# Expert weights on two DMA queues, a slot table made on chip, and empty slots left out of the row transfers

## The reference, cut to what matters

```
x  = x + mixed @ w_out
h2 = rmsnorm(x)
group  = argmax over 8 of (h2 @ w_rg + b_rg)             # top-1 group
2 experts of the group's 8 by (h2 @ w_re + b_re)         # top-2
wts = softmax over the two, times the group's probability
y  = sum over the 2 of wts * ((silu(h2 @ w_gate[e]) * (h2 @ w_up[e])) @ w_down[e])
out = rmsnorm(x + y)
```

## Time and profile before

| | us |
|---|---|
| median of 3 runs | 1718.99 (1711.0 to 1719.74) |
| the profiled execution's own time | 1719.11 |
| its span | 1717.2 |
| mixer, to the last transposes of mixed | 977 |
| w_out, routing, to the first turn_x | 977 to 1128 |
| expert loop | 1128 to 1681 |
| tail | 1681 to 1717.2 |
| mean granted TensorE clock | 0.901 of full |

### The profile page before, as it was taken

The page is one execution under the profiler, slowest core; times in us unless marked ns, Lnnn a source line. Parts: engine busy times, 40 slices in busy tenths (PEclk is TensorE's granted clock), DMA queues, the critical chain, the costliest instruction groups (busy, mean ns, idle before and its releaser), DMA issues.

```text
span 1717.2 us, 20700 instructions
## 1 busy us (share of the span) xinstructions
PE 1419.1 (83%) x6772; PEld 809.0 (47%) x6772; DVE 822.1 (48%) x1718; ACT 334.2 (19%) x901; POOL 205.3 (12%) x301
## 2 busy tenths in 40 slices
PE   5799999999999999999999698267786878778780
PEld 4458567475574755757557543222222222222220
DVE  2286575866857657577476323512222122212224
ACT  3122122232231312313123201001111111101112
POOL 2210121101211111101111000210000000000002
PEclk9899899999989989999899699579988898989895
DMA  8931030210302103021012320359999999999985
GB/s 187 193 100 38 26 87 15 61 38 26 87 14 62 38 26 86 3 74 38 26 25 110 122 87 25 150 210 421 421 423 421 423 422 423 421 423 422 422 366 181
DMA packets 127246, 306.61 MB, mean 179 GB/s; under 512 B 15564, under 2 KB 89254, under 8 KB 102246
## 3 DMA queue, kind: packets, MB, share of 16 engines
q1 hardware_dynamic: 111750, 258.87, 40.1%
q0 software_dynamic: 8800, 27.52, 4.5%
q10 hardware_dynamic: 6672, 19.93, 4.1%
HBM read 272.45 MB, written 34.83 MB: 179 GB/s over the span
## 4 chain that ended last, share of the span: by engine, by line
PE 61%; DMA 23%; DVE 7%; issue 3%; ACT 3%; SPq 1%; POOL 0%; POOLq 0%; ACTq 0%; DVEq 0%
DMA arena<-in_w_up 22%; PE PB L1081 13%; PE PB L1099 10%; PE PB L1415 8%; PE PB L1105 7%; PE PB L1359 4%; PE PB L1183 2%; PE PB L1211 2%; PE PB L1076 2%; DVE arena L1561 1%; PE PB L1074 1%; PE PB L1299 1%; PE PB L1290 1%; PE PB L1125 1%; PE PB L1038 1%
## 5 line engine op out<-in xcount | busy, mean ns | idle before, releaser
L1415 PE MATMUL PB<-arena 128*64 128x512 f32 x1024 | 269.3, 675 | 115.7 <-DMA arena<-in_w_up 111.8
L1081 PE MATMUL PB<-arena 128*128 128x512 f32 x512 | 224.0, 595 | 0.0
L1415 PEld LDWEIGHTS PB<-arena 128*64 128x64 f32 x1024 | 76.7, 154 | 282.6 <-issue 143.3
L1914 DVE TENSOR_SCALAR arena<-arena 128x256 f32<-128x256 f32 x32 | 9.4, 295 | 383.5 <-ACT arena L953 383.5
L1105 PE MATMUL PB<-arena 128*128 128x128 f32 x1280 | 169.4, 288 | 6.2 <-ACT arena L841 5.5
L1099 PE MATMUL PB<-arena 128*128 128x384 f32 x512 | 170.8, 487 | 0.0
L1105 PEld LDWEIGHTS PB<-arena 128*128 128x128 f32 x1280 | 158.4, 201 | 14.7 <-ACT arena L841 7.4
L902 ACT ACTIVATE arena<-PB 128x512 f32<-128x512 f32 (+3 forms) x116 | 60.0, 521 | 483.8 <-PE PB L1423 256.1
L1081 PEld LDWEIGHTS PB<-arena 128*128 128x128 f32 x512 | 96.0, 190 | 118.6 <-issue 118.1
L1099 PEld LDWEIGHTS PB<-arena 128*128 128x128 f32 x512 | 95.4, 190 | 63.2 <-issue 3.8
L1435 PE MATMUL PB<-arena 128*64 128x512 f32 x512 | 116.9, 598 | 1.1 <-ACT arena L902 1.1
(11 more groups left out here) (412 smaller groups left out, 1994.7 us busy)
## 6 DMA issues: line engine op xcount, KB each, us to landing
arena<-in_w_gate SPq DMA_DIRECT2D x64, 1024.0 KB, 19.4
arena<-in_w_up SPq DMA_DIRECT2D x64, 1024.0 KB, 21.5
arena<-in_w_down SPq DMA_DIRECT2D x64, 1024.0 KB, 25.2
arena<-in_w_in SPq DMA_DIRECT2D x58, 512.0 KB, 6.3
ye_d<-arena ACTq DMA_DIRECT2D x32, 512.0 KB, 8.1
Sb<-in_state_dn SPq DMA_DIRECT2D x8, 512.0 KB, 4.1
ye_d<-arena SPq DMA_DIRECT2D x2, 2048.0 KB, 8.9
out<-Sb POOLq DMA_DIRECT2D x8, 512.0 KB, 3.9
```

The lines of the kernel that those rows point to most:

```text
L1081: last = mm(PB[g][:, :], wch[:, c, g, :], hT[:, c, 0:TP], start=c == 0, stop=c == KC - 1)
L1415: last = mm(gu_bank[a][half[k], :], xT[:, a, c, half[k]], wgu[a][:, k, :, c, :], start=c == 0, stop=c == KC - 1)
```

## The change

There are six edits.

1. The expert loop's up loads move from SP to ACT. ACT issues the two of pair j+3 inside follow(j), after the exponential of pair j+1 and before it copies the transposed rows of pair j+2. SP keeps gate and down, and waits once for `s_ov_done` ahead of its second group of loads.
2. The slot table is made on chip. One-hot masks of the rank (`oh`) times one-hot masks of the expert scaled by (token number + 1) give, by small matmuls into PB[2], the number of the token in each slot and 0 in an empty one. `row_numbers` turns that into two index lists: `gidx` for the gather and `yidx` for the store. An empty slot has the index 4095 and is out of bounds in both.
3. Gathers get `bounds_check=T - 1, oob_is_err=False`. The store of the results is now an indirect scatter by POOL, out of bounds for empty slots, into `y2_d`, where row t (first choice) or 1024 + t (second) belongs to a token. The junk fill of `ye_d` is gone.
4. The overflow blocks still use a table in HBM; its arithmetic (`overflow_slots`) and the pair weights (`pair_weights`) move on DVE behind turned(0, 1), inside the start of the expert loop, and POOL's 10 small scatters go behind its first four gathers.
5. In the routing stage `ranks(n)` and `slot_table(n)` are done tile by tile, ACT's `stats(n)` goes ahead of its copy for tile n-1, DVE's resid(n) and h2_rows(n) go ahead of logits(n-1) and choose(n-1), and out_rows(4) is cut in four groups of 256 columns whose 32 output rows lie in four partition groups of one bank.
6. In the tail SP loads both rows of each token with one direct DMA per tile into five buffers, and no store waits for the one before.

```
+            def up_weights(it, a):
+                j = it * 2 + a
+                act.wait_ge(s_gu_ps, 1 + j)
+                for k in range(2):
+                    act.dma_start(wgu[a][:, k, 1, :, :], w_up[ds(it * 4 + (2 * a + k)), :, :]...).then_inc(gu_in[a], 16)
-            def follow(it, a, nxt=True, turn=True):
+            def follow(it, a, nxt=True, turn=True, up=True):
                 hid_turned(it, a)
                 if nxt:
                     exp_gate(*later(it, a, 1))
+                if up:
+                    up_weights(*later(it, a, 3))
                 if turn:
                     turned(*later(it, a, 2))
                 rows_out(it, a)
...
+            def gather(it, a):
+                j = it * 2 + a
+                pool.wait_ge(s_xt_ps, 1 + j * 2)
+                pool.tensor_copy(gidx2[:, a:a + 1], gidx[:, ds(j)]).then_inc(s_idx_ready, 1)
...
+                pool.indirect_dma_start(X[:, a, :], None, h2_d[:, :], bass.IndirectOffsetOnAxis(ap=gidx2[:, a:a + 1], axis=0),
+                                        bounds_check=T - 1, oob_is_err=False).then_inc(X_in[a], 16)
+            def scatter(it, a):
...
+                pool.indirect_dma_start(y2_d[:, :], bass.IndirectOffsetOnAxis(ap=yidx2[:, a:a + 1], axis=0), ys[:, a, :], None,
+                                        bounds_check=2 * CODE - 1, oob_is_err=False).then_inc(ye_out[a], 16)
+            for j in range(4):
+                gather(j // 2, j % 2)
+            pool.wait_ge(s_ov_done, 1)
+            (10 indirect DMAs into slot_d)
+            with pool.Fori(0, NPAIR // 2 - 2) as it:
+                for a in range(2):
+                    gather(it + 2, a)
+                    scatter(it, a)
...
+            def slot_table(n):
+                pe.wait_ge(s_oh_done, n + 1)
+                for k in range(2):
+                    for a in range(2):
+                        last = mm(PB[2][CAP * a:CAP * a + CAP, 0:NPAIR], oh[:, n, k, :], M[:, n, 3 + k, a:NE:2], ...)
...
             for n in range(NT):                       # PE
                 out_rows(n)
+                if n >= 2:
+                    ranks(n - 2)
                 if n:
                     route_rows(n - 1)
+            for n in range(NT - 2):
+                slot_table(n)
             route_rows(NT - 1)
+            ranks(3), ranks(4), slot_table(3), slot_table(4)
...
+                    for q in range(4):                # out_rows(4)
+                        last = mm(PB[0][32 * q:32 * q + 32, 0:256], hT[:, c, TP:T], wo[:, c, q * 256:(q + 1) * 256], ...)
...
+            for n in range(NT):                       # ACT
+                stats(n)
+                if n:
+                    h2_turned(n - 1)
...
             turned(0, 1)                              # DVE
+            pair_weights()
+            overflow_slots()
...
+            for n in range(NT):                       # SP, tail
+                sp.dma_start(yg[0:R, n, :, :], y2_rows[n * P:n * P + R, :, :]).then_inc(yg_in[min(n, 2)], 16)
```

More of the change, by code:

```diff
@@ L562, in _ @@
                 load_down(0, k, k)
-            sp.wait_ge(s_route_done, 1)
             def gate_up_weights(it, a):
@@ L577, in _ @@
                 gate_up_weights(it, 0)
+                sp.wait_ge(s_ov_done, 1)
                 down_weights(it - 1, 1)
@@ L925, in _, with stats @@
                 cpa(hT[:, 0:4, n * P:n * P + R], PB[2 * (n % 2)][:, :].rearrange("p (c k) -> p c k", c=4)[:, :, 0:R]).then_inc(s_mT_act, 1)
-            for n in range(NT):
+            def stats(n):
                 R = rows_of[n]
@@ L991, in further @@
                 rows_out(it, a)
[L993 to L997, removed]
+            further_blocks(act, further)
             for n in range(NT):
@@ new lines, in _, with row_numbers @@
+            resid(0)
+            h2_rows(0)
+            for n in range(1, NT):
+                resid(n)
+                if n >= 2:
+                    one_hot_ranks(n - 2)
+                h2_turned(n - 1)
+                h2_rows(n)
+                logits(n - 1)
+                if n == NT - 1:
+                    h2_turned(n)
+                choose(n - 1)
+            logits(NT - 1)
+            choose(NT - 1)
+            one_hot_ranks(NT - 2)
+            one_hot_ranks(NT - 1)
+            def row_numbers(v, em, sf, th, o):
+                step(ts(em, v, 0.0, 4.0 * CODE, ALU.is_equal, ALU.mult))
+                ch.inc(stt(sf, v, -1.0, em, ALU.add, ALU.add))
+                step(ts(th, v, CODE + 1.0, -1.0 * CODE, ALU.is_ge, ALU.mult))
+                ch.inc(cp(yidx[:, o], sf))
+                step(tt(gidx[:, o], sf, th, ALU.add))
+                dve.sem_inc(s_route_done, 1)
@@ L1837, in _ @@
+            cnt, ova, ovb, ov, adj, eb, ec = (e64[:, k, :] for k in range(1, 8))
+            dve.wait_ge(s_rk_ps, NT + 1)
+            row_numbers(PB[2][:, 0:NPAIR], adj[:, 0:NPAIR], adj[:, NPAIR:], eb[:, 0:NPAIR], slice(0, NPAIR))
+            ch.inc(cp(rkS[:, 0:NP, :].rearrange("p n e -> p (n e)"), PB[4][:, 0:NP * 64]))
+            step(cp(rkS[:, NP:, :].rearrange("p n e -> p (n e)"), PB[3][:, 0:128]))
+            cnt = rkS[:, NT, :]
             step(ts(ov, cnt, float(CAP), None, ALU.is_gt))
@@ L1937, in _ @@
             turned(0, 1)
-            with dve.Fori(0, NPAIR // 2 - 1) as it:
+            pair_weights()
+            overflow_slots()
+            for a in range(2):
+                follow(0, a)
+            with dve.Fori(1, NPAIR // 2 - 1) as it:
                 for a in range(2):
@@ L1947, in further @@
                 rows_out(it, a)
+            dve.wait_ge(s_slots_moved, 32)
+            step(cp(ovf[:, 0, :], ovraw[:, :]))
+            row_numbers(*(ovf[:, k, :] for k in range(4)), slice(NPAIR, NBLK // 2))
             further_blocks(dve, further)
```

324 lines of the change are left out of this document (170 added, 154 removed).

## The result

The kernel after takes 1662.05 us in the median (1659.5 to 1663.34), the kernel before 1719.37 beside it: ratio 0.9672, 95% interval 0.9636 to 0.9708. The forecast was 1630 with a range of 1604 to 1660. The direction was right, the size too large: 57 us are gained where 89 were forecast, and the time lies 2 us past the range. The profiled execution has a span of 1661.6 us.

A forecast was written before the change was run, and what follows sets the result against it. The prediction took DMA to bound the expert loop at about 422 GB/s. Its terms, -55.6 - 30.7 + 3.5 + 1 - 7.4 = -89.2, took 1719.1 to 1630 us, with a range of 1604 to 1660.

The forecast's parts named there:

- What bounds the loop: Expert loop: DMA bounds it at about 422 GB/s, 34.8 us a turn, and keeps the bound after the change.
- at 422 GB/s 55.6 us: Expert loop: skipping empty slots saves 23.5 MB of gathers and stores, 55.6 us; bounds 0 and 55.6.
- POOL's 10 scatters (12.7 us) are hidden: Start of the expert loop: the small scatters cost nothing, since gather(4) is wanted 20 us later.
- the hole of DMA: Start of the expert loop: DMA idle from about 21.5 to 25 us after turn_x(0), +3.5 us, bounds 0 and 8.
- Edit 6, the tail, -7.4: Tail after the loop: shortened from 33.1 to 25.7 us, so -7.4, bounds -10 and -4.
- DVE without a break: Tail: after issue and first tile, VectorE runs its steps without stopping, 20.3 us.
- The routing stage, -30.7: Routing ahead of the loop: -32.5 - 5.4 + 7.2 = -30.7 us, bounds -46 and -21; turn_x(0) at 1097.
- Edit 1, 0: Expert loop: issuing up loads from ACT gains 0, as the DMA engines are never out of work.
- the store from POOL, +1: Result stores issued by POOL: 0 in the loop, about +1 us once at the last pair.
- A: Rival for gathers and stores: out-of-bounds rows are moved or replaced all the same; 1686 us, chance 0.10.
- C: Rival in the loop: ACT is held inside its own DMA issues, slower than before; 1772 us, chance 0.04.
- B: Rival in the loop: three queues with work at once slow the engines to 400 GB/s; 1656 us, chance 0.07.

The follow-up runs named there:

- e7: Kernel after, with a bound on the ten small scatters so nearly all their 4-byte writes are left out: 1646.95 us, ratio 0.9583.
- e1: Kernel after without POOL's ten small scatters of the overflow table and their wait: 1644.96 us, ratio 0.9575.
- e8: Kernel after with ranks spread over the slots, the small scatters' writes bounded and a semaphore for every tile of the tail: 1632.83 us, ratio 0.9494.
- e4: Kernel before with only the up loads moved to ACT: 1716.17 us, ratio 0.9994.
- e2: Kernel after with the up loads back on SyncE, behind the gate loads: 1667.55 us, ratio 0.9689.
- e3: Kernel after without the ten small scatters, up loads back on SyncE, and the final norm's weight loaded ahead of the tail's tiles: 1654.71 us, ratio 0.961.
- e9: Kernel after with spread ranks, bounded scatters, a semaphore per tail tile, and up loads back on SyncE: 1636.91 us, ratio 0.9525.
- e5: Kernel after with an expert's ranks spread over its 64 slots by a table in place of the iota: 1649.69 us, ratio 0.9583.
- e6: Kernel after with ranks packed, eight in a row on the eight partitions of one engine: 1693.5 us, ratio 0.9833.

## Why the prediction was too low

1. **What bounds the loop.** Right, with a gap: DMA bounds it before and after. The text measured DMA as one resource of 422 GB/s. It behaves as sixteen of 26.4, and the turn ends with the busiest.
2. **Edit 3, "at 422 GB/s 55.6 us".** This is the step that failed. The bytes were right (27% of each transfer moves), the size was not: the sentence "The rate must not fall with the mix" rested on weights alone, which load all engines alike. In the kernel after the filled rows sit on some eight to ten engines. A turn took 32.5 us and not 31.05. Spreading the same rows took 12.5 us off the loop (15 to 20 by the expectation), packing them added 29.1 (33 by the expectation). The text gave this term the bounds 0 and 55.6, but its range took it at 55.6 throughout; with any smaller part of it the range would have had to reach further up.
3. **Edit 4, "POOL's 10 scatters (12.7 us) are hidden".** The second failed step. GpSimd's time is hidden, as the text says, and the hole of DMA that it forecast at +3.5 is there (326 and 289 GB/s from 1107 to 1127 us make 20 - (13 x 326 + 7 x 289) / 422 = 5.2 us). But the writes were costed by their bytes, at nothing, and slowed everything beside them: 9.7 us (e7) to 12.4 (e1). The wait for `s_ov_done` came as forecast: SyncE's down loads went out 29.5 us after turn_x(0), 29 by the text.
4. **Edit 6, the tail, -7.4.** It gave 33.1 - 29.2 = 3.9. "DVE without a break" was wrong: the third tile waited 2.82 us, since three tiles share one semaphore, and the first step came 7 us after the first issue and not 5.4. With one semaphore per tile the end comes 2.8 us sooner (e8).
5. **The routing stage, -30.7.** turn_x(0) came within 2 us (1095.12 against 1097), in part by luck: the stage began 2.0 us later than in the kernel before. From out_rows(0) on it took 108.5 us and not 143.4, so -34.9. The stalls behind stats are 2.35 to 2.78 us, as costed at 2.4. The clock behind them was not costed: out_rows(2) and (3) take 15.64 and 15.29 us for 13.95, at a granted clock of 0.89 and 0.91, 3.0 us more. out_rows(4) took 5.97 us and not 8.5, and most of that at the lower clock; by the estimate of 3.6 us at the full clock four groups do run abreast, which the text priced at 3.5 and did not take. The Trainium skill's "TensorE: Matmul & The Clock Gate", section "Part 3: Packing small matmuls", from which the text estimated 4.4 us, is nearer to that than the value taken. The stretch behind choose(4) gave 2.6 us more than forecast (1085.79 to 1095.12, 9.3 us and not 11.9).
6. **Edit 1, 0.** Right in the kernel before (e4, 0.9994). In the kernel after, two queues fill a hole at the loop's start worth 2.5 to 6 us of the loop (e2, e3, e9), which the text did not see: with one queue the up loads stand behind the wait for `s_ov_done` that edit 4 brought.
7. **Edit 3, the store from POOL, +1.** Nothing in the loop waits for it in any trace. Right in kind.
8. **The rivals.** A is out: q0 moved 5.74 MB in 20 pairs. C is out: ScalarE's issues took 348 ns. B has the right time, 1656 against 1662, by a wrong mechanism. Its rate of 400 GB/s is what the steady part shows, but not for the number of queues: one queue gives 409 (e2), and two queues with spread rows give 418 (e5).
9. **The sums.** Two do not come out quite. The stated bounds of the terms add up to 1608 to 1648 and not 1604 to 1650, and the steps of the tail to 20.2 and not 20.3. Neither changes the account.

The loop's 32.8 us over the forecast are then: imbalance and scatters together 534.8 - 511.6 = 23.2 (e8, with both gone), and 9.6 that remain in e8. Of these, 418 against 422 GB/s over some 470 us make 4.5, and the hole of 1107 to 1127, 4.5 us in e8 by the same working as in point 3, makes 1. Whether the 418 come from the engines that still have 3 rows where others have 2 or from the packets of skipped rows, no run here separates. The packet records give the second a size: in e8 some 3800 skipped rows of 9 ns are 35 of 5232 engine-us, 0.7%, where 418 lacks 1% of 422 (an estimate). The last 4 us are open.

## What to carry to other kernels

When an indirect transfer leaves rows out, ask where the remaining rows lie. The turns here went by the busiest of sixteen engines, so spread valid rows over all partition groups; one table of ranks did it, for 12 us. Some thousand 4-byte writes to HBM cost 10 to 12 us beside a stream of weights, though their issue was hidden: bound them, as e7 does, or try them in a quiet stage or on chip. A wait added to a queue holds up everything behind it, not only the load that needs it. Where a new order makes TensorE wait, look at its granted clock behind the wait too. And a sum of bytes over a mean rate should be checked once per engine before it is trusted.

## What the runs showed of the hardware

- A skipped (out-of-bounds) row of an indirect DMA moves no bytes but keeps its packet: 145 packets a transfer with 34 of 128 rows filled. q0's packets of 40 transfers took 5.1% of 5232 us, with the moved rows.
- Which partitions are filled is worth 44 us between e5 and e6, at equal instructions and bytes. The packed order was laid out by the assignment that e6's expectation names, and gave the time of eight rows on the busiest engine, as that assignment asks.
- 1088 writes of 4 bytes, in ten scatters, doubled the mean time of the weights' packets beside them (0.28 to 0.59 us), over some 20 us, and landed after 12.0 us. The median 8 KB packet stayed at 0.31 us, and 98 of 715 took 1 to 4.46 us.
- Four groups of 32-row matmuls, 64 records of 256 columns, took 5.97 us at a granted clock of 0.60, some 3.6 at the full clock, where the same columns in 32 records of 512, one after the other, took 13.85 at 1.00: 3.8 times at equal clock, an estimate.
- Behind waits of 2.4 to 2.8 us between stretches of matmuls the granted clock of out_rows(2) to (4) was 0.89, 0.91 and 0.60. In the kernel before, with waits of 0.8 us in the same places, it stayed at 1.00.
